# One compression stage of a two-block transformer: inner product with operands swapped, clears ahead of the last bias row, output weights behind the bias rows

## The reference

```python
kc, vc = ...                      # keys and values to compress: 256 tokens, 4 groups of 64
starts = arange(15) * 16          # n_c = 15 blocks of 32 tokens
def compress(t, pe, w1, w2):
    blk = t[:, tok_idx] + pe      # 15 blocks x 4 groups, 2048 numbers each
    return gelu(blk @ w1) @ w2    # w1: 2048 x 256, w2: 256 x 64
k_cmp, v_cmp = compress(kc, pe_k, w1_k, w2_k), compress(vc, pe_v, w1_v, w2_v)
s = einsum('bsgrd,bngd->bgrsn', q, k_cmp) * scale + bias_c
p_cmp = masked_softmax(s)         # 16 heads x 256 tokens x 15 blocks
o_cmp = einsum(p_cmp, v_cmp)
o = g0 * o_cmp + g1 * o_sel + g2 * o_win
return o @ w_out                  # a_w_out, 1024 x 1024
```

## Time and profile before

| | us |
|---|---|
| median of 3 runs | 1337.48 (1337.18 to 1340.62) |
| the profiled execution's own time | 1338.87 |
| its span | 1337.1 |
| TensorE busy (weight loads) | 1303.7 (1089.3), 98% (81%) |
| VectorE busy | 815.8, 61% |
| ScalarE busy | 653.7, 49% |
| POOL busy | 257.9, 19% |

### The profile page before, as it was taken

One profiled execution on the slowest core, in us unless ns is written; L12 is line 12 of the kernel. 1 busy time (PEld: TensorE's weight loads), 2 busy tenths in 40 slices (PEclk: granted clock), 3 DMA queues, 4 the chain that ended last, 5 costly groups with the idle time before them and its releaser, 6 DMA issues. The chain is left out here.

```text
span 1337.1 us, 19355 instructions
## 1 busy us (share of the span) xinstructions
PE 1303.7 (98%) x7309; PEld 1089.3 (81%) x7309; DVE 815.8 (61%) x1219; ACT 653.7 (49%) x956; POOL 257.9 (19%) x337
## 2 busy tenths in 40 slices
PE   6998999999999999999999999999999999999997
PEld 5996788888799988888888788888977767888886
DVE  3448765555564486654556755557888757655554
ACT  4328654444443377543444654446443664544442
POOL 5410110000000021102000589501375120200000
PEclk9999999999999999999999999999999999999999
DMA  9980555555455653567755565654534334665561
GB/s 294 255 143 6 154 172 192 185 187 189 144 192 187 161 129 98 163 213 164 231 189 166 177 191 188 216 187 143 189 126 158 97 124 144 199 191 188 185 190 51
DMA packets 155659, 225.82 MB, mean 169 GB/s; under 512 B 13027, under 2 KB 107467, under 8 KB 155596
## 3 DMA queue, kind: packets, MB, share of 16 engines
q1 hardware_dynamic: 141008, 208.36, 49.8%
q0 software_dynamic: 9840, 11.60, 4.2%
q10 hardware_dynamic: 4748, 5.01, 1.2%
HBM read 223.59 MB, written 1.27 MB: 168 GB/s over the span
## 5 line engine op out<-in xcount | busy, mean ns | idle before, releaser
L597 DVE TENSOR_TENSOR units_lo<-raw_units,units_hi 128x2048 fp32r<-128x2048 f32 x96 | 222.2, 2314 | 154.7 <-ACT units_hi L551 154.7
L197 PE MATMUL bank<-units_hi,turned_hi 128*128 128x512 f32 (+1 forms) x792 | 307.2, 388 | 3.3 <-DVE units_lo L180 1.3
L199 PE MATMUL bank<-units_hi,turned_lo 128*128 128x512 f32 (+1 forms) x792 | 302.0, 381 | 0.0
L198 PE MATMUL bank<-units_lo,turned_hi 128*128 128x512 f32 (+1 forms) x792 | 301.8, 381 | 0.0
L180 DVE TENSOR_TENSOR units_lo<-raw_units,units_hi 128x2048 fp32r<-128x2048 f32 (+2 forms) x103 | 232.7, 2267 | 111.6 <-ACT units_hi L172 111.5
L172 ACT ACTIVATE units_hi<-raw_units 128x2048 fp32r<-128x2048 f32 (+2 forms) x103 | 193.0, 1885 | 120.5 <-PE bank L199 86.8
L551 ACT ACTIVATE units_hi<-raw_units 128x2048 fp32r<-128x2048 f32 x96 | 183.5, 1912 | 103.8 <-PE bank L199 95.6
L197 PE MATMUL bank<-units_hi,second_hi 128*128 128x512 f32 (+1 forms) x560 | 218.5, 390 | 0.4 <-ACT rows L2277 0.4
L199 PE MATMUL bank<-units_hi,second_lo 128*128 128x512 f32 (+1 forms) x560 | 216.5, 387 | 0.0
L198 PE MATMUL bank<-units_lo,second_hi 128*128 128x512 f32 (+1 forms) x560 | 216.3, 386 | 0.0
L197 PEld LDWEIGHTS bank<-units_hi,turned_hi 128*128 128x128 f32 x792 | 149.1, 188 | 34.5 <-issue 3.1
(11 more groups left out here) (346 smaller groups left out, 1834.3 us busy)
## 6 DMA issues: line engine op xcount, KB each, us to landing
raw_units<-in_ffn_w_up SPq DMA_DIRECT2D x88, 512.0 KB, 4.7
raw_units<-in_ffn_w_in SPq DMA_DIRECT2D x88, 512.0 KB, 4.7
raw_units<-in_ffn_w_down SPq DMA_DIRECT2D x22, 1024.0 KB, 5.0
raw_units<-in_ffn_w_out SPq DMA_DIRECT2D x22, 1024.0 KB, 4.9
raw_units<-in_w_in SPq DMA_DIRECT2D x18, 1024.0 KB, 5.1
raw_units<-in_b_w_q SPq DMA_DIRECT2D x12, 1024.0 KB, 5.1
raw_units<-in_a_w_in SPq DMA_DIRECT2D x10, 1024.0 KB, 11.5
raw_units<-in_kv_w SPq DMA_DIRECT2D x6, 1024.0 KB, 5.1
```

The source lines that it names most:

```text
L197: pe.matmul(out, lh, rh, start=start, stop=False, skip_group_check=True)
L198: pe.matmul(out, lh, rl, start=False, stop=False, skip_group_check=True)
L199: return pe.matmul(out, ll, rh, start=False, stop=True, skip_group_check=True)
L597: dve.tensor_tensor(m.WL[:, slot(n0 + j), :], m.RAW[:, slot(n0 + j), :], m.WH[:, slot(n0 + j), :].bitcast(F32), ALU.subtract).then_inc(m.l ...
```

## The change

The inner layer swaps its operands: the blocks (64 columns, 15 of each 16 in use, the sixteenth cleared) are stationary and the weights move, 256 columns; K writes partitions 0 to 63 and V 64 to 127 of bank 4, in turn, and TensorE waits for both halves of the blocks. One gelu over 128 x 256 then does both; two transposes and one copy turn the result. The first score pair moves ahead of `compress_keys_tensor`. POOL clears HID and PC before the last bias row instead of after it, and waits for the one product only. The two output matrices are loaded in four DMAs of 128 partitions each per unit, and SP issues the first attention's only when all 16 bias rows have landed.

```diff
-    units.extend([("a_out", 2, ULEN)] * 4)
+    units.extend([("a_out", 4, ULEN)] * 4)        # and the same for b_out
...
     project_gate_a_tensor(pe, m, n + 8)
-    compress_keys_tensor(pe, m)
+    hidden_turn_tensor(pe, m)
     pe.wait_ge(m.s("a_left_out"), 4)
     pe.wait_ge(m.s("a_right_out"), 4)
     score_pair_a_tensor(pe, m, 0)
-    pe.wait_ge(m.s("gelu1_steps"), 1)
+    compress_keys_tensor(pe, m)
     project_keys_a_part(pe, m, n + 9, 4, 0, 0)
...
     for n, (dst, src) in enumerate(((m.A.RK, m.A.KC2), (m.A.RV, m.A.VC2))):
+        pool.memset(dst[:, :, :, NCMP:16], 0.0)
...
-    bias_a_gpsimd(pool, m, range(10, HEADS))
-    pool.wait_ge(m.s("a_products_made"), 2)
+    bias_a_gpsimd(pool, m, range(10, 15))
+    pool.wait_ge(m.s("a_products_made"), 1)
     pool.memset(m.A.HID, 0.0).then_inc(m.s("padding_zero"), 1)
     pool.memset(m.A.PC, 0.0).then_inc(m.s("padding_zero"), 1)
+    bias_a_gpsimd(pool, m, range(15, HEADS))
...
-    for n, (w1, r) in enumerate(((m.A.W1K, m.A.RK), (m.A.W1V, m.A.RV))):
-        pe.wait_ge(m.s("blocks_ready"), n + 1)
-        for u in range(16):
-            for k in range(2):
-                ins = mm(pe, m.pb[4 + n][:, k * 64:k * 64 + KV * NCMP], w1[:, u, k * P:(k + 1) * P],
-                         r[:, u, :, :].rearrange("p g n -> p (g n)"), u == 0 and k == 0, u == 15)
+    pe.wait_ge(m.s("blocks_ready"), 2)
+    for u in range(16):
+        for n, (w1, r) in enumerate(((m.A.W1K, m.A.RK), (m.A.W1V, m.A.RV))):
+            ins = mm(pe, m.pb[4][n * DH:(n + 1) * DH, 0:S], r[:, u, :, :].rearrange("p g n -> p (g n)"), w1[:, u, :],
+                     u == 0, u == 15)
...
+def hidden_turn_tensor(pe, m):
+    pe.wait_ge(m.s("gelu0_steps"), 6)
+    for k in range(2):
+        ins = pe.transpose(m.pb[5][:, k * P:(k + 1) * P], m.A.GX[:, k * P:(k + 1) * P], m.IDENT[:, :])
+    ins.then_inc(m.s("a_products_made"), 1)
...
-    gelu_vector(dve, m, "gelu0", m.A.GX, m.A.GY, hidden(0), m.A.GH[:, :, 0:60])
-    gelu_vector(dve, m, "gelu1", m.A.GX, m.A.GY, hidden(1), m.A.GX)
+    gelu_vector(dve, m, "gelu0", m.A.GX, m.A.GY, m.pb[4][:, 0:S], m.A.GX)
+    dve.wait_ge(m.s("a_products_made"), 2)
+    dve.tensor_copy(m.A.GH, m.pb[5][:, 0:S]...).then_inc(m.s("hidden_copied"), 1)
+    # spread_hidden_vector: waits hidden_copied and padding_zero, two copies into HID as before
...
-    rows = w.rearrange("(g a r d) n -> g a d r n", g=2, a=2, r=4)
+    rows = w.rearrange("(g a r d) n -> g r a d n", g=2, a=2, r=4)
-            load_unit(sp, m, n, [(raw[a * DH:(a + 1) * DH], rows[G, a, :, :, c * 512:(c + 1) * 512])
-                                 for a in range(2)])
+            load_unit(sp, m, n, [(m.RAW[:, slot(n), r * 512:(r + 1) * 512],
+                                  rows[G, r, :, :, c * 512:(c + 1) * 512]) for r in range(4)])
...
             project_a_sync(sp, m)
+            sp.wait_ge(m.s("bias_a_in"), 16 * HEADS)
             out_sync(sp, m, "a_out", i["a_w_out"][0])
```

More of the change, by code:

```diff
@@ L109, in plan_units @@
         block("b_in")
-    units.extend([("b_out", 2, ULEN)] * 4)
+    units.extend([("b_out", 4, ULEN)] * 4)
     ffn(1)
@@ L1118, in project_a_vector @@
     compress_hidden_vector(dve, m)
+    spread_hidden_vector(dve, m)
     split_lo(dve, m, first_unit("a_out"))
@@ L1136, in compress_gpsimd @@
     for n, (dst, src) in enumerate(((m.A.RK, m.A.KC2), (m.A.RV, m.A.VC2))):
+        pool.memset(dst[:, :, :, NCMP:16], 0.0)
         for g in range(KV):
             blocks = bass.AP(src.tensor, src.offset + g * S, [list(src.ap[0]), [2, 16], [16, NCMP]])
-            ins = pool.tensor_tensor(dst[:, :, g, :], blocks,
+            ins = pool.tensor_tensor(dst[:, :, g, 0:NCMP], blocks,
                                      m.PE[:, n, :].unsqueeze(2).to_broadcast([P, 16, NCMP]), ALU.add)
@@ L1143, in compress_gpsimd @@
     pool.memset(m.A.SC[:, 0, :, m.ncmp[0]:16], NEG).then_inc(m.s("padding_zero"), 1)
-    bias_a_gpsimd(pool, m, range(10, HEADS))
-    pool.wait_ge(m.s("a_products_made"), 2)
+    bias_a_gpsimd(pool, m, range(10, 15))
+    pool.wait_ge(m.s("a_products_made"), 1)
     pool.memset(m.A.HID, 0.0).then_inc(m.s("padding_zero"), 1)
     pool.memset(m.A.PC, 0.0).then_inc(m.s("padding_zero"), 1)
+    bias_a_gpsimd(pool, m, range(15, HEADS))
 def compress_hidden_tensor(pe, m):
     pe.wait_ge(m.s("w1_in"), 32)
-    for n, (w1, r) in enumerate(((m.A.W1K, m.A.RK), (m.A.W1V, m.A.RV))):
-        pe.wait_ge(m.s("blocks_ready"), n + 1)
-        for u in range(16):
-            for k in range(2):
-                ins = mm(pe, m.pb[4 + n][:, k * 64:k * 64 + KV * NCMP], w1[:, u, k * P:(k + 1) * P],
-                         r[:, u, :, :].rearrange("p g n -> p (g n)"), u == 0 and k == 0, u == 15)
-        ins.then_inc(m.s("a_products_made"), 1)
+    pe.wait_ge(m.s("blocks_ready"), 2)
[8 more added lines that the diff above has]
+        ins = pe.transpose(m.pb[5][:, k * P:(k + 1) * P], m.A.GX[:, k * P:(k + 1) * P], m.IDENT[:, :])
+    ins.then_inc(m.s("a_products_made"), 1)
 def compress_keys_tensor(pe, m):
-    pe.wait_ge(m.s("gelu0_steps"), 6)
+    pe.wait_ge(m.s("hidden_copied"), 1)
     pe.wait_ge(m.consts_in, 16 * m.n_consts)
     for k in range(2):
-        ins = mm(pe, m.pb[6][:, 0:60], m.W2[:, 0, k, :], m.A.GH[:, k, 0:60], k == 0, k == 1)
+        ins = mm(pe, m.pb[6][:, 0:DH], m.W2[:, 0, k, :], m.A.GH[:, k, 0, :], k == 0, k == 1)
     ins.then_inc(m.s("k_cmp_made"), 1)
@@ L1228, in compress_keys_scalar @@
     act.wait_ge(m.s("padding_zero"), 1)
-    src = m.pb[6][:, 0:60].rearrange("p (g n) -> p g n", g=KV)
+    src = m.pb[6][:, 0:DH].rearrange("p (g n) -> p g n", g=KV)
     for par in range(2):
         rows = slice(par * DH, (par + 1) * DH)
-        ins = act.activation(m.A.KCB[rows, :, par, 0:NCMP], src[rows, par::2, :], ACT.Copy)
+        ins = act.activation(m.A.KCB[rows, :, par, 0:NCMP], src[rows, par::2, 0:NCMP], ACT.Copy)
     ins.then_inc(m.s("k_cmp_ready"), 1)
-    gelu_scalar(act, m, "gelu1", m.A.GY)
 def compress_weights_scalar(act, m):
@@ L1257, in compress_hidden_vector, with spread_hidden_vector @@
 def compress_hidden_vector(dve, m):
-    def hidden(n):
-        return m.pb[4 + n][:, 0:P].rearrange("p (k c) -> p k c", k=2)[:, :, 0:60]
     dve.wait_ge(m.s("a_products_made"), 1)
-    gelu_vector(dve, m, "gelu0", m.A.GX, m.A.GY, hidden(0), m.A.GH[:, :, 0:60])
-    dve.wait_ge(m.s("gelu0_steps"), 6)
+    gelu_vector(dve, m, "gelu0", m.A.GX, m.A.GY, m.pb[4][:, 0:S], m.A.GX)
     dve.wait_ge(m.s("a_products_made"), 2)
-    gelu_vector(dve, m, "gelu1", m.A.GX, m.A.GY, hidden(1), m.A.GX)
-    dve.wait_ge(m.s("gelu1_steps"), 6)
+    dve.tensor_copy(m.A.GH, m.pb[5][:, 0:S].rearrange("p (k n c) -> p k n c", k=2, n=2))\
+        .then_inc(m.s("hidden_copied"), 1)
+def spread_hidden_vector(dve, m):
+    dve.wait_ge(m.s("hidden_copied"), 1)
     dve.wait_ge(m.s("padding_zero"), 3)
     for k in range(2):
-        src = m.A.GX[:, k, :].rearrange("p (g n) -> p g n", g=KV)
+        src = m.A.GH[:, k, 1, :].rearrange("p (g n) -> p g n", g=KV)[:, :, 0:NCMP]
         ins = dve.tensor_copy(m.A.HID[:, k, :, :, 0:NCMP], src.unsqueeze(2).to_broadcast([P, KV, 4, NCMP]))
@@ L1484, in out_sync @@
     n = first_unit(stage)
-    rows = w.rearrange("(g a r d) n -> g a d r n", g=2, a=2, r=4)
+    rows = w.rearrange("(g a r d) n -> g r a d n", g=2, a=2, r=4)
     for c in range(2):
         for G in range(2):
-            raw = m.RAW[:, slot(n), :].rearrange("p (r c) -> p r c", r=4)
-            load_unit(sp, m, n, [(raw[a * DH:(a + 1) * DH], rows[G, a, :, :, c * 512:(c + 1) * 512])
-                                 for a in range(2)])
+            load_unit(sp, m, n, [(m.RAW[:, slot(n), r * 512:(r + 1) * 512],
+                                  rows[G, r, :, :, c * 512:(c + 1) * 512]) for r in range(4)])
             n += 1
@@ L3224, in views @@
     A.CD = cut.take(TT, HEADS)
-    A.GX = cut.take(2, 60)
-    A.GY = cut.take(2, 60)
-    A.GH = cut.take(2, 60)
+    A.GX = A.VCR.rearrange("p g d -> p (g d)")
+    A.GY = cut.take(S)
+    A.GH = cut.take(2, 2, DH)
     A.NM = cut.take(NPA, 2, 2)
@@ L3244, in views @@
     cut = Cutter(rows, 0)
-    A.RK = cut.take(16, KV, NCMP)
-    A.RV = cut.take(16, KV, NCMP)
+    A.RK = cut.take(16, KV, 16)
+    A.RV = cut.take(16, KV, 16)
     cut = Cutter(rows, 0)
```

## The result

| | before | after |
|---|---|---|
| time, median (lowest to highest) | 1338.45 us (1337.18 to 1340.62) | 1372.56 us (1368.92 to 1374.46) |
| profiled execution: time, span | 1338.87, 1337.1 | 1368.92, 1367.1 |
| granted clock, mean | 0.996 | 0.986 |
| predicted | | 1334.5 (1331.9 to 1339.5) |

The ratio is 1.0246, 95% interval [1.0234, 1.0258]: the change costs 2.5%, where I forecast a gain of 3 us. The 30.0 us between the two spans arise in two places only, as the start of the same split of a weight unit in both traces shows: 14.2 us are there from the first attention on (the second output unit is split at 165.6 instead of 151.4), 1.0 of it is given back about 375 us, and 16.8 come in the second attention (30.0 from its output projection to the end).

A forecast was written before the change was run, and what follows sets the result against it. TensorE, busy nearly throughout, and the chain of bias rows and weights to L1282 both had to shrink; row 16, load and splits put L1282 at 92.1 against 95.11, so 1337.48 - 3.0 = 1334.5 us, range 1331.9 to 1339.5.

The forecast's parts named there:

- Inner layer: TensorE's swapped compression layer: 32 pairs of 256-column passes take 7.0 us, plus 0.1 for a change of form.
- Both block sets: TensorE waits for K's and V's blocks and two small memsets, ending at 66.8; it idles 1.5 us.
- One gelu: The single gelu on 256 columns takes 3.0 us, from 74.1 to 77.1; TensorE idles 0.3.
- Memsets ahead of the row: POOL's two memsets wait for the product (74.1) and end at 76.0; the spread ends by 79.2.
- Row 16: The last bias row goes out at 76.6, after the earlier rows have landed, and lands 5.4 us later at 82.0.
- The load: First output-weight unit, 1 MB in four pieces by 128 partitions: 5.6 us (5.0 to 7.2), in at 87.6.
- From the load to L1292: Split hi 1.9 us, split lo's start to this line 2.5, handing over 0.1: it starts at 92.1.
- Output weights of the other attention: Loading them by 128 partitions costs 0 (between -0.3 and +0.3), as unit 0 is split 9 us after landing.
- The gain, had the load had all engines: The whole change: L1282 starts at 92.1 against 95.11, so the kernel is 3.0 us faster.
- the case without gain: Rival: row 16 near 84.5 or a load of 7 us or more gives 1337; chance 14%.
- four pieces one after another: Objection from the skill's bandwidth rule: the four quarters in series take an estimated 10.4 us, a loss of 1.8.

The follow-up runs named there:

- e1: The changed kernel with both output matrices loaded as before (two DMAs of 64 partitions a unit), SP's wait for the bias rows kept; 1338.36 us, ratio 1.0007.
- e7: The changed kernel with the output weights' rows read in another order, 128 rows in one outermost loop; computes other numbers; 1338.58 us, ratio 1.0002.
- e9: The kernel of e1 without SP's wait for the 16 bias rows; 1340.81 us, ratio 1.0016.
- e3: The kernel before with one part alone, both output matrices in four DMAs of 128 partitions a unit; 1355.72 us, ratio 1.0124.
- e10: The kernel before with the swapped inner layer and sixteen-column blocks alone; POOL's order, SP's order and loads as before; 1340.00 us, ratio 1.0008.
- e11: The kernel of e1 with the first output-weight unit's split moved behind the softmax of the compressed scores on ScalarE and VectorE; 1333.94 us, ratio 0.9975.
- e8: The kernel of e1 with SP's wait set to POOL's last clear instead of the 16th bias row's landing; 1336.30 us, ratio 0.9985.

## Why the prediction was wrong

- *Inner layer* (7.0 us and 0.1): 7.16. Right: 0.22 us a pair, so the column halves do run side by side, and no weight load is added on top.
- *Both block sets* (end 66.8): POOL's last addition ends at 66.3. The size is right; that TensorE starts at 66.69 is luck, for the 1.5 us of idle time that I forecast in front of it is not there: in this trace it works on the unit before until then. In e1 and e7 it waits 0.5 and 1.2 us for the blocks.
- *One gelu* (3.0 us): 4.0, from 73.90 to 77.88. One step took 1.10 us, 0.29 in e9. TensorE waits 1.2 us for it instead of 0.3, and the keys unit starts at 79.6, not 78.8. The term was too small, but it is off the path.
- *Memsets ahead of the row*: right; the spread ran at 78.87.
- *Row 16* (out 76.6, in 82.0): 76.54, and 5.3 us later in. Right, and with it the reading that it waits for the rows before it: row 16 goes out about 0.5 us after row 15 has landed, in after (76.0) as in e3 (81.1, row 16 at 81.57) and in e9 (90.3, row 16 at 90.80), and e10, where the rows share the queues as before, waits 19.5 us again.
- ***The load* (5.6 us, 5.0 to 7.2): 23.2. This is the step that failed.** I priced a transfer by its bytes and its partitions, from rows whose sources all had 64 or 128 turns outside, and did not write out the loops of the new source. "DMA: Bandwidth & Descriptors" of the Trainium skill, section Why a DMA increments its semaphore by 16 and not by 1, says that the number of engines is the largest up to 16 that divides the slowest dimension longer than 1 of both sides; that is 2 here, and the traces agree (share 0.14, 0.26, 0.52 for 2, 4, 8). I weighed the Trainium skill's 1 MiB (same page, section Bandwidth) and not this rule. By rows alone the upper bound of 7.2 had no ground either, since no row showed a source of this form.
- *From the load to L1292* (4.5): 4.3. Right.
- *Output weights of the other attention* (0, between -0.3 and 0.3): 16.8. The same error, at the first unit (5.2 us) and at the last. The 9 us between landing and split are cover for a load of 7 us, not for four that take some 20 each.
- *The gain, had the load had all engines* (3.0): 0.5 of span in e1, nothing measurable in e7. In series the load takes 7.0 to 7.4, against my 5.6. The next units' transfers follow it at once, but that is not what makes e1's slow: its two transfers landed 5.1 and 6.6 us behind their issues, and the same pair of b_w_out in before 4.9 and 6.5, where the next one left 5 us later. For the old form, then, the 7.2 that I had as upper bound was the nearest row; I had given the case without gain 14%. In e7 the fourth transfer is issued 1.3 us behind the first and lands 5.6 us later.

The second half of the answer to this last point is TensorE's clock. In e1 and e7 it waits up to 1.6 us between 95 and 105 for results of VectorE and ScalarE, and then works at a lower clock. The same stretch of e1, e7 and e11, TensorE busy throughout in all three:

```profile
105.00:110.00 5.00, 5.00 (x33) 3.40 (x33) 2.83 (x18) 4.30 (x19) 0.00 (x0) 0.74 0.00 0
```

```profile
105.00:110.00 5.00, 5.00 (x26) 3.50 (x26) 3.01 (x21) 4.45 (x19) 0.00 (x0) 0.56 0.00 0
```

```profile
105.00:110.00 5.00, 5.00 (x46) 3.53 (x44) 3.42 (x21) 3.68 (x14) 0.00 (x0) 1.00 0.01 3
```

With 33 and 26 products instead of 46 in 5 us, e1 loses an estimated 1.4 us in it and e7 2.2. That is as large as what was left of the gain at L1292 (0.7 us in e1, 0.6 in e7, about 1 us more if one counts from the start of POOL's blocks). The forecast had no term for this.

No rival named the mechanism. What stood nearest, four pieces one after another at an estimated 10.4 us, asked about the size of a transfer and would have cost 4.8 us.

## What to carry to other kernels

Before a load is rewritten, write out the loops of both sides after joining those that are evenly spaced: with an outermost loop of 2, 4 or 8 these transfers of 256 KB by 128 partitions ran at the rate of as many DMA engines. A load that loses its lead is priced by what it takes in series, from its first issue to its last landing. And where an in-order engine handles data for later in front of work that is due now, moving that handling back can be worth more than making the data come sooner (spans of one execution each): against e1, whose kernel both change, e8 gained 2.2 us of span and e11 4.6.

## What the runs showed of the hardware beyond that

- *A neighbour slows VectorE.* The same step on 256 columns (L1222) took 1.10 us in after, where POOL's memset of 0.96 began at 74.81 with it, and 0.29 in e9, where POOL's last memset had ended 0.04 us before (0.30 in e10, where no memset ran). The two spreading copies took 1.12 us beside a memset in before and 0.48 in after.
- *A short wait can cost clock.* In e10 TensorE was idle 3.5 of 15.3 us and got 0.79 of its clock in the 9.7 us of full work behind (in before 1.00). In e9 it waited 3.15 us in front of 97.62 and got 0.62 from 100 to 105, in e7 1.56 in front of 102.89 and got 0.56 from 105 to 110. In before and e11, where no wait from 80 to 125 is longer than 0.97, it kept 1.00. Making TensorE's work shorter without what it waits for gained nothing.
- *All 16 engines were slower each.* 297 GB/s is 18.6 an engine, or 20.4 for the 14.6 that the share counts as busy, against 24 to 26 with 2 to 8. What limits them is not settled; no run tells it.
- Not separated: how much of e7's 7.0 us is the unit's own load, and how much the units issued right behind it. For e1's form the pair in before answers it, with at most 0.2 us.
